# A two-block transformer forward pass: 32x32 diagonal blocks of the first mixer's triangular inverse formed on GpSimd, and the order of work around it

## The reference, cut to what matters

```python
a = jnp.where(strict, jnp.einsum("bhncd,bhnjd->bhncj", k_beta, k) * decay, 0.0)
t_inv = lax.linalg.triangular_solve(eye + a, jnp.broadcast_to(eye, a.shape), left_side=True, lower=True)
u = jnp.einsum("bhncj,bhnjv->bhncv", t_inv, v_beta)
...
v_new = u_c - jnp.einsum("bhck,bhkv->bhcv", w_c, state)
out = jnp.einsum("bhck,bhkv->bhcv", qd_c, state) + jnp.einsum("bhcj,bhjv->bhcv", qk_c, v_new)
```

## Time and profile before

| what | value |
|---|---|
| runs | 1420.28, 1413.04, 1413.71 us (median 1413.71) |
| profiled execution, first to last instruction | 1411.1 us |
| median of the runs less that span | 2.6 us |
| PE busy | 1395.7 us, 99% of the span |
| DVE, ACT, POOL busy | 920.5, 728.4, 21.1 us |
| granted PE clock | 1.000 of full speed, mean |
| DMA | 216.61 MB, mean 154 GB/s |

### The profile page before, as it was taken

One profiled execution on the slowest core, in us unless ns is written; L12 is line 12 of the kernel. 1 busy time (PEld: TensorE's weight loads), 2 busy tenths in 40 slices (PEclk: granted clock), 3 DMA queues, 4 the chain that ended last, 5 costly groups with the idle time before them and its releaser, 6 DMA issues.

```text
span 1411.1 us, 19872 instructions
## 1 busy us (share of the span) xinstructions
PE 1395.7 (99%) x7787; PEld 1193.6 (85%) x7787; DVE 920.5 (65%) x1620; ACT 728.4 (52%) x1249; POOL 21.1 (1%) x44
## 2 busy tenths in 40 slices
PE   9999999999999999999999999999999999999999
PEld 8999999988888888888888888788888887888887
DVE  7867777747655548666555499875554588655543
ACT  7664646335544436545444365755444467454441
POOL 3000000000100000000000000000000000000000
PEclk9999999999999999999999999999999999999999
DMA  8533332225666555436565555246665541465552
GB/s 238 149 102 91 84 96 77 74 90 164 206 185 191 181 171 156 150 116 197 181 192 181 177 164 180 75 129 214 181 191 185 162 163 61 126 214 183 188 186 88
DMA packets 168838, 216.61 MB, mean 154 GB/s; under 512 B 11219, under 2 KB 136746, under 8 KB 168746
## 3 DMA queue, kind: packets, MB, share of 16 engines
q1 hardware_dynamic: 166976, 213.03, 48.8%
q10 hardware_dynamic: 1770, 2.32, 0.5%
HBM read 214.26 MB, written 1.05 MB: 153 GB/s over the span
## 4 chain that ended last, share of the span: by engine, by line
PE 86%; DVE 10%; ACT 2%; issue 1%; DMA 1%; SPq 0%; ACTq 0%; DVEq 0%
PE psum L898 23%; PE psum L900 23%; PE psum L899 23%; PE psum L1118 4%; DVE w_low L646 3%; PE psum L1110 2%; PE psum L1124 1%; PE psum L1288 1%; PE psum L1248 1%; PE psum L1321 1%; PE psum L889 1%; DVE work L818 1%; PE psum L1092 1%; DVE work L2409 1%; PE psum L1307 1%
## 5 line engine op out<-in xcount | busy, mean ns | idle before, releaser
L646 DVE TENSOR_TENSOR w_low<-ring,w_high 128x1024 fp32r<-128x1024 f32 (+3 forms) x395 | 473.6, 1210 | 316.8 <-ACT w_high L632 316.4
L632 ACT ACTIVATE w_high<-ring 128x1024 fp32r<-128x1024 f32 (+3 forms) x395 | 410.6, 1049 | 432.8 <-PE psum L900 419.0
L898 PE MATMUL psum<-w_high,hT 128*128 128x512 f32 (+2 forms) x944 | 371.8, 394 | 0.0
L900 PE MATMUL psum<-w_high,hT 128*128 128x512 f32 (+2 forms) x944 | 366.1, 388 | 0.0
L899 PE MATMUL psum<-w_low,hT 128*128 128x512 f32 (+2 forms) x944 | 365.5, 387 | 0.0
L900 PEld LDWEIGHTS psum<-w_high,hT 128*128 128x128 f32 x944 | 177.2, 188 | 36.5
L898 PE MATMUL psum<-w_high,parts 128*128 128x512 f32 (+1 forms) x532 | 207.9, 391 | 0.0
L899 PEld LDWEIGHTS psum<-w_low,hT 128*128 128x128 f32 x944 | 177.5, 188 | 33.8
L898 PEld LDWEIGHTS psum<-w_high,hT 128*128 128x128 f32 x944 | 177.4, 188 | 34.0 <-DVE work L2409 0.3
L900 PE MATMUL psum<-w_high,parts 128*128 128x512 f32 (+1 forms) x532 | 206.0, 387 | 0.0
L899 PE MATMUL psum<-w_low,parts 128*128 128x512 f32 (+1 forms) x532 | 205.8, 387 | 0.0
(11 more groups left out here) (282 smaller groups left out, 1396.5 us busy)
## 6 DMA issues: line engine op xcount, KB each, us to landing
ring<-in_ffn_w_gate_up SPq DMA_DIRECT2D x176, 256.0 KB, 3.2
ring<-in_w_gate_up SPq DMA_DIRECT2D x176, 256.0 KB, 3.2
ring<-in_gdn_w_in SPq DMA_DIRECT2D x48, 512.0 KB, 3.8
ring<-in_ffn_w_down SPq DMA_DIRECT2D x44, 512.0 KB, 3.3
ring<-in_w_down SPq DMA_DIRECT2D x44, 512.0 KB, 3.3
ring<-in_da_w_qkv SPq DMA_DIRECT2D x24, 512.0 KB, 3.9
ring<-in_gdn_w_out SPq DMA_DIRECT2D x16, 512.0 KB, 3.3
ring<-in_mla_w_out SPq DMA_DIRECT2D x8, 512.0 KB, 3.9
```

The costliest lines, as they stand in the source:

```text
L632: nc.scalar.activation(piece_slot(w_high, n), piece_slot(ring, n), ACT.Copy).then_inc(s.w_hi, 1)
L646: nc.vector.tensor_tensor(piece_slot(w_low, n), piece_slot(ring, n), piece_slot(w_high, n).bitcast(F32), ALU.subtract).then_inc(s.w_lo, 1)
L898: mm(out, lhs[0], rhs[0], start=start, stop=False)
L900: return mm(out, lhs[1], rhs[0], start=False, stop=stop)
```

## The change

- A group's matrices are negated when they are formed (`minus_beta`), kept in one of two buffers (`g_ats`), and stored by SP to device memory as whole matrices. SP then loads the 32 diagonal blocks of 32x32 (2 chunks x 4 heads x 4 blocks) into 32 partitions, one block in each partition.
- GpSimd inverts them by forward substitution (`inverse_of_blocks`): for j = 1 to 30 a product of j rows by 31-j columns, and an addition of the same size, each waiting for the one before. It sets the diagonal, copies the result transposed, issues two transfers of the blocks to device memory into zeroed whole matrices, waits, waits for the group before to have read `g_x` and `g_y`, loads both as whole matrices (512 KB each), and waits for them before it turns to the next group.
- TensorE does the last step (32 to 128) alone: `crossed`, `first_order`, `second_order`, `third_order`. The transposes `turned_y`, the copies `copy_x`, level 0 and two of three steps are gone, and two of three mask transposes.
- The order is rewritten: tiles 10 to 19 and all `z` quarters of group 0 come before the inverse of group 0 is used; the tail holds the `z` quarters of the next group; `products` of the next group come before `crossed`; two output pieces (0 and 1) come before the last tail, which holds pieces 2 to 5. Key tables are loaded late, after GpSimd's last stores.

```diff
+            def inverse_of_blocks(g):
+                u, step = squares_of(blocks, g), of_group(block_step, g)
+                pool.wait_ge(s.blocks_loaded, 16 * (g + 1))
+                for j in range(1, SUB - 1):
+                    later = SUB - 1 - j
+                    m = step[:, 0:j * later].rearrange("p (c n) -> p c n", n=later)
+                    own(tt(m, u[:, 0:j, j:j + 1].to_broadcast([GROUP_BLOCKS, j, later]),
+                           u[:, j:j + 1, j + 1:SUB].to_broadcast([GROUP_BLOCKS, j, later]), ALU.mult))
+                    own.wait()
+                    own(tt(u[:, 0:j, j + 1:SUB], u[:, 0:j, j + 1:SUB], m, ALU.add))
+                    own.wait()
+                own(gp.memset(of_group(blocks, g)[:, 0:SUB * SUB:SUB + 1], 1.0))
+                own.wait()
+                own(copy(squares_of(turned_blocks, g).rearrange("p c n -> p n c"), u))
+                own.wait()
+                pool.dma_start(y_blocks, u).then_inc(s.images_stored, 16)
+                pool.dma_start(x_blocks, squares_of(turned_blocks, g)).then_inc(s.images_stored, 16)
+                pool.wait_ge(s.images_stored, 32 * (g + 2))
+                if g:
+                    pool.wait_ge(s.u_psum, 2 * g)
+                pool.dma_start(matrices(g_x), x_whole).then_inc(s.inverse_loaded, 16)
+                pool.dma_start(matrices(g_y), y_whole).then_inc(s.inverse_loaded, 16)
+                pool.wait_ge(s.inverse_loaded, 32 * (g + 1))
...
+        KEYS_AT = [tile_piece[i] for i in (15, 20, 24)] + [z_piece[3][3] + 5]
...
             for n, (k, cols, src) in enumerate(pieces):
+                if n in KEYS_AT:
+                    g = KEYS_AT.index(n)
+                    sp.wait_ge(s.at_ready, g + 1)
+                    if g:
+                        sp.wait_ge(s.blocks_loaded, 16 * g)
+                    sp.dma_start(keys_whole, matrices(g_ats[g % 2])).then_inc(s.keys_stored, 16)
+                if n - 1 in KEYS_AT:
+                    g = KEYS_AT.index(n - 1)
+                    sp.wait_ge(s.keys_stored, 16 * (g + 1))
+                    sp.dma_start(squares_of(blocks, g), keys_blocks).then_inc(s.blocks_loaded, 16)
                 if n >= RING:
                     sp.wait_ge(s.w_lo, n - RING + 1)
...
+            def crossed(g):
+                pe.wait_ge(s.inverse_loaded, 32 * (g + 1))
...
+                for t in range(T):
+                    each_head(g, t, g_ats[g % 2], lambda t, h: g_x[:, t, h, :], by_head, s.p_psum)
...
-                turned_y(g, 1)
-                for step in range(STEPS):
-                    inverse_step(g, step)
-                    if step < STEPS - 1:
-                        for t in range(T):
-                            pe.wait_ge(s.gy_ready, g_step(g, step, t))
-                            turned_y(g, t)
-                    beside_level(g, 2 * step + 2)
```

More of the change, by code:

```diff
@@ L1111, in heads, with each_head @@
                 last.then_inc(done, 1)
[L1113 to L1119 removed]
+            def each_head(g, t, lhs, rhs, of_bank, done):
+                for h in range(GH):
+                    last = mm(of_bank(B[t])[:, h], lhs[:, t, h, :], rhs(t, h), start=True, stop=True)
+                last.then_inc(done, 1)
@@ L1209, in group @@
+                if g:
+                    turned_outputs(g - 1, 2)
+                crossed(g)
+                first_order(g)
+                second_order(g)
+                if g and more:
+                    tile(at + 7)
+                elif not more:
+                    output_piece(1)
+                third_order(g)
+                pe.wait_ge(s.gy_ready, g_tile(g, 1))
                 pe.wait_ge(s.vt_ready, 4 * g + 4)
@@ new lines, in _ @@
+            rope_angles()
+            tiles(9)
+            silu(4)
+            copy_v(0)
+            tiles(10)
+            tiles(11)
+            silu(5)
+            z_pieces(0, 0)
+            gate_diff(1)
+            tiles(12)
+            z_pieces(0, 1)
+            gate_exp(1)
+            squares_kq(1)
+            tiles(13)
+            silu(6)
+            z_pieces(0, 2)
+            tiles(14)
+            z_pieces(0, 3)
+            z_silu(0)
+            tiles(15)
+            silu(7)
@@ new lines, in _ @@
+            tiles(16)
+            tiles(17)
+            silu(8)
+            tiles(18)
+            tiles(19)
+            silu(9)
+            copy_w(0)
+            state_copied(0)
+            z_pieces(1, 0, 1)
+            z_pieces(1, 2, 3)
+            z_silu(1)
+            copy_v(1)
+            output_squares(0)
+            gate_diff(2)
+            tiles(20)
+            gate_exp(2)
+            squares_kq(2)
+            tiles(21)
+            silu(10)
+            tiles(22)
+            outputs_high(0, 2)
@@ new lines, in _ @@
+            copy_w(1)
+            tiles(23)
+            silu(11)
+            state_copied(1)
+            z_pieces(2, 0, 1)
+            z_pieces(2, 2, 3)
+            z_silu(2)
+            copy_v(2)
+            output_squares(1)
+            tiles(24)
+            tiles(25)
+            silu(12)
+            gate_diff(3)
+            tiles(26)
+            tiles(27)
+            gate_exp(3)
+            silu(13)
+            tiles(28)
+            squares_kq(3)
+            tiles(29)
+            silu(14)
@@ new lines, in _ @@
+            tiles(30)
+            outputs_high(1, 2)
+            copy_w(2)
+            tiles(31)
+            silu(15)
+            state_copied(2)
+            z_pieces(3, 0, 1)
+            z_pieces(3, 2, 3)
+            z_silu(3)
+            copy_v(3)
+            output_squares(2)
+            output_pieces(0)
+            outputs_high(2, 2)
+            copy_w(3)
+            output_pieces(1)
+            state_copied(3)
+            output_pieces(2, 3, 4, 5)
+            act.wait_ge(s.images_stored, 32 * (GROUPS + 1))
@@ new lines, in _, with z_pieces, output_pieces, keys_made @@
+            split_low(dve, tile_piece[7] + SPLIT)
+            other_scales(0)
+            def z_pieces(g, *which):
+                for r in which:
+                    split_low(dve, z_piece[g][r] + SPLIT)
+            def output_pieces(*which):
+                for n in which:
+                    split_low(dve, a_gout.first + n + SPLIT)
+            def keys_made(g):
+                gate_causal(g)
+                key_scales(g)
+                key_products(g)
+            def first_crossed(g):
+                for t in range(T):
+                    dve.wait_ge(s.p_psum, g_tile(g, t))
+                    tt(g_p[:, t, :, :], by_head(B[t][:, :]), below(GH), ALU.mult).then_inc(s.p_ready, 1)
```

572 lines of the change are left out of this document (289 added, 283 removed).

## The result

The changed kernel takes **1445.5 us** (median of 4 runs, 1444.7 to 1448.7) against 1413.7 of the kernel before (4 runs beside it, 1413.0 to 1420.3): ratio 1.0213, 95% interval 1.0183 to 1.0243. The forecast was 1448.

A forecast was written before the change was run, and what follows sets the result against it. GpSimd's inversion chain was taken as the bound: start 66, four groups of 40.5, losses 49.3, transfers 4 x 12 put the last `crossed` at 325.3 us, 31.9 past break-even; with small terms 1448 us, range 1405 to 1490.

The forecast's parts named there:

- TensorE relieved: Two of three inversion steps and all three sets of transposes go in each group: 71.6 us less TensorE work.
- GpSimd's start: Group 0's matrices, stored by SP at piece 20 and loaded back as blocks, let GpSimd begin at 66 us.
- transfers of a group: GpSimd's two stores and two loads after the copy, in its own line: 12 us, between 7.3 and 16.2.
- The arithmetic: GpSimd's 60 dependent operations a group: 2.18 ns an element, 0.18 us fixed, 0.09 gap; 37.8 us, 40.5 with copy and diagonal.
- the rivals: GpSimd keeps up and the kernel is faster, 0.14; no change that can be told, 0.06; weight stream stalls, within the forecast.
- The losses beside VectorE: GpSimd operations meeting VectorE's splits lose 0.98 us each; with gatings 49.3 us over four groups, 24.6 if half are hidden.
- The later groups' blocks are loaded during the group before and don't bind: Blocks of groups 1 to 3 were to be ready before GpSimd turns to them, so no waiting was counted.
- I cost it at nothing: ACT's and VectorE's share of the removed steps goes too; both had room, so it was priced at zero.
- no-wait floor of 1342: The kernel's time with 71.6 us of TensorE work gone and no new wait: about 1342 us.
- The weight stream: SP's stores and loads share the weights' queue, so late key products could stall weights; no price, chance within the forecast's.
- The restart after idling: TensorE restarts slowly after idling, as at the start of the program: some 2 us.
- break-even of 293.4: Start of the last `crossed` at which the change neither gains nor loses: 287.8 + 5.7 = 293.4 us.

The follow-up runs named there:

- e1: Changed kernel with GpSimd's substitution loop cut to its first two steps (4 operations a group instead of 60), output not the reference's: 1397.9 us.
- e6: Changed kernel with earlier first keys and tiles, outputs' transposes behind second-order products, VectorE gating before making keys, last two groups' keys stored a piece later: 1437.4 us.
- e9: From e6: VectorE's and ScalarE's orders changed, copy of crossed blocks ahead of a split, keys made before gating, later place of last keys taken back: 1434.0 us.
- e11: From e9: keys of groups 2 and 3 two pieces later in SP's queue, last products made earlier: 1423.2 us, ratio 1.0038 to the kernel before.
- e5: Changed kernel with unread matmuls filling TensorE's three longest kinds of wait, nothing moved: 1442.9 us.
- e7: Kernel before the change with 125 more unread matmuls ahead of its first projection, running some 26 us later: 1446.5 us.
- e8: Kernel before the change with 133 unread matmuls ahead of its first projection: 1440.3 to 1440.9 us in three of four executions, 1445.2 in one.

## Why the prediction came out right, and which steps were wrong

The time came out within 2.5 us of the forecast, and slower was given 0.80. But the sum was right through errors that offset each other, and by my own test it fails: I wrote that the prediction is wrong as a whole if the periods are under 57 us. They average 56.0. The last 7.5 us, which bring the total so near the forecast, aren't the changed mixer's, and no term of the forecast stands for them: the closeness is luck.

| term | forecast | measured |
|---|---|---|
| TensorE relieved | 71.6 us | 610 instructions gone; the size wasn't measured apart |
| GpSimd's start | 66 | 66.5 |
| a group's undisturbed operations, with diagonal and copy | 40.5 | 34.9 + 2.3 |
| lost beside VectorE, four groups | 49.3 | 26.3 |
| transfers of a group | 12 (7.3 to 16.2) | 11.0, 12.4, 13.2, 12.2 |
| waiting for blocks | 0 | 24.3 |
| last `crossed` begins | 325.3 | 314.8 |
| from there to 1150 us, more than before | 3 | 4.5 |
| behind that | 0 | 7.5 |
| span more than before | 34.9 | 33.1 |

**The arithmetic** (term mis-sized). From 30 to 240 elements the undisturbed products took 0.23 to 0.61 us, which is 1.8 ns an element and 0.18 fixed, and the additions up to 0.64 (2.0 ns an element), not 2.18; the gap between two was 0.07 to 0.08, not 0.09. The bound above, that short rows cost 0.1 more, did not come true: 30 elements took 0.23 us. Two side values of the rivals were also added up wrongly: with a fifth of the losses hidden the terms give 1420, not 1422, and with none at all 1380, not 1377.

**The losses beside VectorE** (mechanism right, size half). Group 0's timeline of GpSimd, and below it VectorE's:

```profile
84.90 0.61 POOL L3128 TENSOR_TENSOR vectors<-consts 32x238 f32<-32x238 f32 x1
...
86.31 1.48 POOL L3128 TENSOR_TENSOR vectors<-consts 32x240 f32<-32x240 f32 x1
87.87 1.56 POOL L3131 TENSOR_TENSOR consts<-consts,vectors 32x240 f32<-32x240 f32 x1
89.51 0.61 POOL L3128 TENSOR_TENSOR vectors<-consts 32x240 f32<-32x240 f32 x1
```
```profile
84.32 1.51 DVE L2513 SCALAR_TENSOR_TENSOR work<-psum,convw,work 128x255 f32<-128x255 f32 x3
85.75 1.57 DVE L693 TENSOR_TENSOR w_low<-ring,w_high 128x1024 fp32r<-128x1024 f32 x1
87.48 1.40 DVE L693 TENSOR_TENSOR w_low<-ring,w_high 128x1024 fp32r<-128x1024 f32 x1 [0.16 <-ACT w_high L679]
```

Each split adds 0.9 us to the operation that meets it, as forecast (0.98); the convolution step from 84.3 to 85.8 adds nothing. 37 splits began between GpSimd's first operation and its last landing, where I had counted 38; but only 27 of them fell into its chains (11, 5, 6 and 5), the others where it waited for transfers or blocks. The 35 lengthened operations lost 0.75 us each on average, the short ones beside gatings less. The forecast's lower bound, half of the losses hidden, was the better value. The loss goes both ways, though VectorE had the room: its 47 splits from 50 to 340 us took 1383 ns on average against 1219 before. The Trainium skill ("SBUF — State Buffer", Who interferes with whom) has a VectorE instruction with two SBUF inputs and a GpSimd one that reads SBUF contend for a port pair that is locked exclusively. The trace agrees in kind on both sides: the pair above took 1.48 and 1.57 us.

**"The later groups' blocks are loaded during the group before and don't bind"** (this step failed, and it hid 24.3 us). TensorE made group 3's products at 246 us, in the work that the order puts into group 2's time; VectorE had the matrices at 249.4, and SP's store, behind pieces of weights, came at 252.4. I had followed only the first group's keys. It offset the two terms above (23 and 13 us).

**"I cost it at nothing", for the new waits of TensorE** (failed). I took TensorE's own line to reach the last `crossed` at 221.8 us with 103 us of idling for GpSimd alone. GpSimd's share of the waits was 33.8 us; 44.2 are other waits (36.8 in e1), at `turned_v`, `turned_outputs` and the end of a group. In the changed kernel they mostly overlap with GpSimd's line; e1 lays them bare. The no-wait floor of 1342 doesn't exist in this order of work: with GpSimd almost free it is 1398.

**The weight stream** (a rival that I left without a price). In the changed kernel ScalarE waited 7.9 us for weights in the mixer. In e6 and e9 the same mechanism, SP waiting for keys with a needed piece behind, made TensorE wait up to 13.6 us at a time; in e11 the longest such wait is 3.7.

**The restart after idling** (term mis-sized: 2 us, where filling the waits gave back 4.7 in e5's profile). I had priced one restart, from the program's start. The half-clock stretches in the mixer are many; the one at 1210 us is no restart and comes without the new mixer too.

**What decides.** Without the waits for blocks the last `crossed` would begin near 290.4 us, before my break-even of 293.4. e11 comes near that, with an inverse landed at 289.8, and it is no faster than before, for what the order and the clock take.

## What to carry to other kernels

When work goes to another engine, write down for every later round, not only the first, when its input is made, by which engine and behind what in each queue: the wait for the later groups' input cost nearly as much here as all the interference. A forecast can be right in its total with a wrong profile; compare each term before trusting the next one. A transfer that waits for a result, in the queue that also feeds everything else, belongs behind the pieces that can already go, not ahead of them: that edit, with another beside it, came with 11 us here.

## What was unexpected of the hardware

- TensorE's granted clock fell to the lower level for 20.6 us at 1210 us, with TensorE busy throughout, behind a stage in which it had idled for under 2 us in ten. Whether it falls there changes from one execution to the next: by the mean clock it was there in five of e7's six executions (0.993 or 0.994) and in part in one of e8's four (0.996). It is worth 7.5 us, 0.5% of this kernel. A difference of this size between two kernels may be that alone. What within the chip sets it was not tried.
- A GpSimd-issued transfer keeps GpSimd for 0.8 to 0.9 us to issue, and lands late. Medians from issue to landing, 50 to 340 us, with KB each:

```profile
work<-x_scratch POOLq DMA_DIRECT2D x4, 512.0 KB, 4.9
work<-y_scratch POOLq DMA_DIRECT2D x4, 512.0 KB, 6.2
...
y_scratch<-consts POOLq DMA_DIRECT2D x4, 128.0 KB, 2.9
```

  The Trainium skill ("DMA: Bandwidth & Descriptors", Anatomy of one DMA) gives each a fixed 2.0 us and a term by bytes. An estimate from that page is some 7 us for the four, as two pairs; they took 11.0 to 13.2, so here the measurement decides.
- VectorE's smallest operations (8 elements) also grew beside GpSimd: those of one line took 259 ns on average where before they took 168. Those of them that began while GpSimd stood took 167 to 169 ns; beside it the longest took 523.

```profile
L2300 DVE SCALAR_TENSOR_TENSOR small<-small 128x8 f32<-128x8 f32 x21 | 5.4, 259 | 0.7
```
```profile
L2196 DVE SCALAR_TENSOR_TENSOR small<-small 128x8 f32<-128x8 f32 x24 | 4.0, 168 | 0.8
```
